# Hybrid layer projects residual times norm weights, rstd applied behind PSUM; small projections in column tiles; key sums in four units; turns later

## The chip, the cores and the metric

The kernel runs on one core of a Trainium2 chip. The metric is device time in microseconds (us) of one execution, inputs in HBM, outputs in HBM; lower is better. Engines in the text: PE is TensorE, DVE is VectorE, ACT is ScalarE, POOL is GpSimd, SP is SyncE, which issues the DMAs.

## The reference

Two networks run one after the other on 256 tokens of width 1024 in fp32. The first has two layers (attention, a gating unit, a dilated attention) and isn't touched. The second puts 16 meta tokens ahead (272 tokens) and has two layers, each: half a SwiGLU FFN, a mixer, half a SwiGLU FFN. Layer 0's mixer is the hybrid one:

```python
h = h + 0.5 * swiglu_ffn(rms_norm(h, ffn_norm[0, 0]), ...)
hn = rms_norm(h, mix_norm[0])          # x * rsqrt(mean(x*x) + 1e-6) * gain
# in the mixer:
fq, fk, fv, ff, gqkv, ga, gb, gz = split_cols_2(hn @ w_in, HYB_SIZES)
o_fox = forgetting_attention(...)       # 8 heads of 64, decay from ff
gqkv = silu(causal_depthwise_conv(gqkv, conv_w)); k, q l2-normalised
o_gdn = gated_delta_rule(...)           # 4 heads of 128, decay from ga, beta from gb
o = concat([o_fox, rms_norm(o_gdn, o_gain) * silu(gz)]);  h = h + o @ w_out
```

The columns `ff`, `ga`, `gb` (8 + 4 + 4) are the small projections. Layer 1's mixer is a recurrence (rwkv) and keeps its form. Since rms_norm multiplies each token by one number (rstd), `hn @ w` is also `(x * gain) @ w` times rstd of the token.

## The kernel before, in words

Everything is held transposed: channels on the 128 partitions in KC = 8 chunks, tokens (272 or 256) in the free dimension. Weights come as blocks of 128x1024 (512 KB) through a ring of RING = 4 slots. Each block is split into a high and a low part (`act_split`: a copy on ACT in two halves of 128x512; `dve_split`: the subtraction on DVE), two blocks (SPLIT = 2) ahead of PE: the half for block n waits until PE has finished the same half of block n - 2. Activations are split in the same way (`act_parts`, `dve_parts`). `pe_tile` (L424) then does one 128x128 tile as three matmuls, L426 to L428; a block is 8 tiles, 24 matmuls.

Each engine runs its own hand-written order, and semaphores join them. Around the change:

- The FFN's last two blocks finish their 8 output banks one by one; `dve_ffn_add` adds each to the residual X.
- `act_norm`, `pe_norm`, `dve_mean`, `act_rstd`, `dve_norm` (L529 to L592): squares on ACT, their sum by fp32 matmuls with ones, mean, Ln, Exp, then the normed chunks H. Then the parts MIX_H, MIX_L, and then PE's first block of the hybrid layer.
- FFN stages don't wait for that: their opening (`pe_open` L599, `act_open`, `dve_open`, L598 to L674) multiplies the residual times gain, takes the first two blocks in halves (PAIR: first half of both, then second half of both), and each product is multiplied by rstd when it leaves PSUM. `OPEN` lists the norms that do this (numbers 3, 5, 6, 8: the four FFNs). The first FFN has no adds or splits to weave in and takes another path in the two helpers.
- The hybrid layer: `pe_hybrid_in`, `act_hybrid_in`, `dve_hybrid_in` (L1826, L1943, L2157) are loops over HYB_CH = 28 blocks i, and after `if i == ...` stands the other work of that turn: small projections (i = 2), their rows through log, scan and spread (3 to 7), convolutions (`dve_convolve`, on DVE), key and query sums (10, 11), grams, an inverse by levels (`ax`, `xax`, 14 to 19), the delta rule by chunks (20 to 26), the forgetting attention (`fox_*`, 18 to 26). ACT copies each block's result from one of two PSUM banks to HP (L1948).
- `pe_mix_out` then projects OUT_H, OUT_L, and an FFN follows.

Of the kernel before, what the change touches and what calls it, by code (L numbers as in the profile page):

```python
# [22 lines left out]
ALU = mybir.AluOpType  # L23
# [3 lines left out]
P = 128  # L27
D = 1024
KC = D // P
# [54 lines left out]
def _columns(table):  # L84
# [11 lines left out]
    ("delta_rows", 8 * P), ("delta_cols", 8), ("chunk_mask", 2 * len(R_WIDTHS)), ("restart", S2), ("row_scan", S2),  # L96
# [12 lines left out]
    ("ffn_g", DEPTH * 2 * KC), ("mix_g", DEPTH * KC), ("final2_g", KC), ("hyb_small", KC * T2),  # L109
# [6 lines left out]
def host_constants():  # L116
# [58 lines left out]
    put("delta_rows", sel)  # L175
    put("delta_cols", cut)
# [11 lines left out]
def host_vectors(i, first):  # L188
# [26 lines left out]
    small = np.zeros((D, T2), np.float32)  # L215
    small[:, 0:8], small[:, 32:36], small[:, 64:68] = w[:, 1536:1544], w[:, 3080:3084], w[:, 3084:3088]
    put("hyb_small", small.reshape(KC, P, T2).transpose(1, 0, 2).reshape(P, -1))
# [52 lines left out]
def build(nc, x_in, pos_in, const_in, first_in, vec_in, weights_in, out):  # L270

    ctx = ExitStack()
    with ctx:
# [245 lines left out]
        NORMED = {use: j for j, use in enumerate((0, 1, 2, 4, 7, NORMS))}  # L519
        OPEN = (3, 5, 6, 8)  # L520
# [97 lines left out]
        def act_open(act, job, use, x, n, gain, high, first):  # L618
# [192 lines left out]
        def pe_fox_weigh(pe, j):  # L811
            pe.wait_ge(fox["turned_taken"], max(FOX_AT["pair", j], FOX_AT["tail", j // 2]) + 1)
            if j:
                pe.wait_ge(act_low, KC * JOBS["hybrid", 1] + j)
            for o in range(2):
                h, out_ = 2 * j + o, PS[64 * o:64 * o + 64, 4, 0:S2]
                v, last = FVN[:, :, 64 * h:64 * h + 64], FOX_TAIL * (h % 4) + FOX_TAIL - META
                tail = FOX_TAIL_T[:, j // 2]
                nc.tensor.matmul(out_[:, 0:256], v[:, 0], FOX_T[:, j % 2, o, 0:256], start=True, stop=False)
                nc.tensor.matmul(out_[:, 128:256], v[:, 1], FOX_T[:, j % 2, o, 256:384], start=False, stop=True)  # L820
                nc.tensor.matmul(out_[:, 256:S2], v[:, 0], tail[:, last:last + META], start=True, stop=False)
                nc.tensor.matmul(out_[:, 256:S2], v[:, 1], tail[:, P + last:P + last + META], start=False, stop=False)
                mm = nc.tensor.matmul(out_[:, 256:S2], v[0:META, 2], tail[0:META, 2 * P + last:2 * P + last + META],
                                      start=False, stop=True)
# [170 lines left out]
        def dve_setup(dve):  # L995
            ang, turns, ang2 = arena(SCR, S1), arena(SCR + 256, S1), arena(SCR + 512, S1)
# [633 lines left out]
        HYB_BANKS, GRAM_BANK = 2, 5  # L1630

        def pe_hybrid_block(pe, i):
            block, _ = BLOCKS["mix_in", 0]
            pe_arrived(pe, block + max(i, 1))
            if i >= HYB_BANKS:
                pe.wait_ge(hs["in_taken"], i - HYB_BANKS + 1)
            for k in range(KC):
                if i == 0:
                    pe.wait_ge(act_low, KC * JOBS["hybrid", 0] + k + 1)
# [1443 lines left out]
```

## Time and profile before

| | |
|---|---|
| median of 3 runs | 2021.8 us (2021.31 to 2022.74) |
| the profiled execution | 2023.71 us, span 2021.9 us |
| PE busy | 1894.4 us, 94% |
| DVE busy | 1279.0 us, 63% |
| ACT busy | 1033.5 us, 51% |
| granted TensorE clock, mean | 0.973 of full |
| DMA | 278.13 MB, 138 GB/s |

PE's matmuls overlap, so its rows last longer (0.29 us) than they stand apart (0.126 us at the full clock, 0.227 at half). One row of a fp32 matmul by ones or by a constant is one of two passes. The hybrid layer lies from 854 to about 1050 us of the span; the FFN openings are at 654, 1079, 1282 and 1818 us.

### The profile page before, as it was taken

The numbers are of one execution on the slowest core, as the hardware profiler recorded it, in microseconds if no ns is written. First come the engines' busy times: TensorE is split into PE (matmuls) and PEld (weight loads), VectorE is DVE, ScalarE is ACT, GpSimd is POOL, SyncE is SP. The second block draws the span as 40 slices with busy tenths as digits, with TensorE's granted clock in tenths as the row PEclk, the third lists the DMA queues.
The fourth block names the chain that finished last, engine by engine and source line by source line (L and its number), as shares of the span: only waits on it lengthen the run. The fifth ranks groups of instructions, "written<-read, shape, count | busy, mean of one in ns | idle before, by whom it ended". The sixth has DMA issues, their size and how long they took to land.

```text
span 2021.9 us, 46291 instructions
## 1 busy us (share of the span) xinstructions
PE 1894.4 (94%) x17922; PEld 1805.1 (89%) x17922; DVE 1279.0 (63%) x2593; ACT 1033.5 (51%) x2037; POOL 25.4 (1%) x20
## 2 busy tenths in 40 slices
PE   5999998999997999989999999999989978979998
PEld 5989988989997999988889999899976978869998
DVE  4667675667666666476456664566566755467764
ACT  4555654555654555447355554555445723155553
POOL 0110000110000000000000000000000000000000
PEclk8999998999998999989999999999989989989999
DMA  5544554544553555532225555455542400025664
GB/s 224 154 137 146 156 177 126 157 141 142 159 174 117 168 174 176 164 90 93 64 64 162 170 176 177 144 170 176 177 161 82 127 31 4 4 73 168 186 187 125
DMA packets 75531, 278.13 MB, mean 138 GB/s; under 512 B 8320, under 2 KB 9600, under 8 KB 74752
## 3 DMA queue, kind: packets, MB, share of 16 engines
q1 hardware_dynamic: 75392, 276.12, 44.4%
q8 instruction: 106, 1.74, 0.3%
q14 instruction: 33, 0.27, 0.0%
HBM read 275.04 MB, written 1.05 MB: 137 GB/s over the span
## 4 chain that ended last, share of the span: by engine, by line
PE 81%; DVE 11%; ACT 5%; issue 2%; DMA 0%; DVEq 0%; SPq 0%; ACTq 0%
PE psum L426 22%; PE psum L427 21%; PE psum L428 21%; DVE weights_low L391 3%; ACT weights_high L383 2%; PE psum L2669 1%; PE psum L2652 1%; PE psum L720 1%; PE psum L1750 1%; PE psum L2666 1%; PE psum L564 1%; PE psum L740 1%; PE psum L2610 1%; DVE normed L589 1%; PE psum L2357 1%
## 5 line engine op out<-in xcount | busy, mean ns | idle before, releaser
L391 DVE TENSOR_TENSOR weights_low<-weight_ring,weights_high 128x512 fp32r<-128x512 f32 x996 | 673.9, 692 | 536.0 <-ACT weights_high L383 526.8
L383 ACT ACTIVATE weights_high<-weight_ring 128x512 fp32r<-128x512 f32 x996 | 615.2, 628 | 603.7 <-PE psum L428 601.6
L426 PE MATMUL psum<-ffn_normed_high,weights_high 128*128 128x272 f32 (+1 forms) x1408 | 407.8, 290 | 13.3 <-DVE ffn_normed_low L652 10.0
L428 PE MATMUL psum<-ffn_normed_high,weights_low 128*128 128x272 f32 (+1 forms) x1408 | 405.4, 288 | 0.0
L427 PE MATMUL psum<-ffn_normed_low,weights_high 128*128 128x272 f32 (+1 forms) x1408 | 405.3, 288 | 0.0
L426 PE MATMUL psum<-first_normed_high,weights_high 128*128 128x256 f32 x1216 | 355.6, 292 | 29.8 <-DVE first_normed_low L445 17.7
L427 PE MATMUL psum<-first_normed_low,weights_high 128*128 128x256 f32 x1216 | 342.7, 282 | 0.0
L428 PE MATMUL psum<-first_normed_high,weights_low 128*128 128x256 f32 x1216 | 342.4, 282 | 0.0
L426 PEld LDWEIGHTS psum<-ffn_normed_high,weights_high 128*128 128x128 f32 x1408 | 266.8, 189 | 17.7 <-issue 11.7
L426 PEld LDWEIGHTS psum<-first_normed_high,weights_high 128*128 128x128 f32 x1216 | 233.6, 192 | 44.7 <-issue 26.6
L428 PEld LDWEIGHTS psum<-ffn_normed_high,weights_low 128*128 128x128 f32 x1408 | 266.7, 189 | 0.0
L427 PEld LDWEIGHTS psum<-ffn_normed_low,weights_high 128*128 128x128 f32 x1408 | 266.3, 189 | 0.1
L427 PEld LDWEIGHTS psum<-first_normed_low,weights_high 128*128 128x128 f32 x1216 | 233.4, 192 | 2.1 <-issue 1.9
L428 PEld LDWEIGHTS psum<-first_normed_high,weights_low 128*128 128x128 f32 x1216 | 233.3, 192 | 0.0
L426 PE MATMUL psum<-ffn_inner_high,weights_high 128*128 (+2 forms) x704 | 201.9, 287 | 1.0 <-DVE weights_low L391 0.5
L428 PE MATMUL psum<-ffn_inner_high,weights_low 128*128 (+2 forms) x704 | 201.3, 286 | 0.0
L427 PE MATMUL psum<-ffn_inner_low,weights_high 128*128 (+2 forms) x704 | 201.1, 286 | 0.0
L426 PEld LDWEIGHTS psum<-ffn_inner_high,weights_high 128*128 128x128 f32 x704 | 132.5, 188 | 2.6 <-DVE weights_low L391 1.6
L428 PEld LDWEIGHTS psum<-ffn_inner_high,weights_low 128*128 128x128 f32 x704 | 132.4, 188 | 0.0
L427 PEld LDWEIGHTS psum<-ffn_inner_low,weights_high 128*128 128x128 f32 x704 | 132.4, 188 | 0.0
L1482 ACT ACTIVATE arena<-arena 128x272 f32<-128x272 f32 (+1 forms) x88 | 37.7, 429 | 96.7 <-DVE arena L1518 96.7
L426 PE MATMUL psum<-mixer_high,weights_high 128*128 128x272 f32 x224 | 69.8, 312 | 5.4 <-DVE mixer_low L445 5.4
(423 smaller groups left out, 2891.4 us busy)
## 6 DMA issues: line engine op xcount, KB each, us to landing
weight_ring<-weights_in SPq DMA_DIRECT2D x508, 512.0 KB, 3.7
arena<-first_in SPq DMA_DIRECT2D x1, 2176.0 KB, 13.8
consts<-const_in SPq DMA_DIRECT2D x1, 1828.5 KB, 17.7
arena<-vec_in SPq DMA_DIRECT2D x1, 1536.0 KB, 9.3
arena<-vec_in SPq DMA_DIRECT2D x1, 1152.0 KB, 5.9
residual<-x_in SPq DMA_DIRECT2D x1, 1088.0 KB, 5.2
out<-normed SPq DMA_DIRECT2D x4, 256.0 KB, 2.5
vectors<-vec_in SPq DMA_DIRECT2D x1, 399.0 KB, 6.6
```

What stands on the lines that cost most here:

```text
L383: nc.scalar.activation(WH[:, n % SPLIT, half], W[:, n % RING, half], ACT.Copy).then_inc(weights_high, 1)
L391: nc.vector.tensor_tensor(WL[:, n % SPLIT, half], W[:, n % RING, half], WH[:, n % SPLIT, half].bitcast(F32), ALU.subtract).then_inc(weight ...
L426: nc.tensor.matmul(psum, WH[:, s, cols], high, start=start, stop=False)
L427: nc.tensor.matmul(psum, WH[:, s, cols], low, start=False, stop=False)
L428: return nc.tensor.matmul(psum, WL[:, s, cols], high, start=False, stop=stop)
L564: mm = nc.tensor.matmul(PS[:, bank, 0:n], ONES, SQ[:, k, 0:n], start=(k == 0), stop=(k == KC - 1))
L589: nc.vector.scalar_tensor_tensor(out=dest[:, k, 0:n], in0=x[:, k], scalar=gain[:, k:k + 1], in1=RS[:, 2, 0:n], op0=ALU.mult, op1=ALU.mult)\
L720: mm = nc.tensor.matmul(A.score(h, m, qi), q[r, c, qi * A.t:(qi + 1) * A.t], k[r, c, 0:w], start=True, stop=True)
L740: mm = nc.tensor.matmul(PS[o:o + A.e, A.out_bank(h), kj * A.t:A.n], v[0:A.t, kj, h * A.e:(h + 1) * A.e], A.probs_t(h, kj), start=(kj == 0) ...
L1482: nc.scalar.activation(FFN_GATE[:, u, 0:n], FFN_GATE[:, u, 0:n], ACT.Silu).then_inc(gates_silu, 1)
L1750: mm = nc.tensor.matmul(inv_psum(g, part)[half(o), m - m0], left[half(o), m], right[half(o), m], start=True, stop=True)
L2357: mm = nc.tensor.matmul(PS[row:row + width, bank, 0:S2], LI[:, k, at:at + width], x[:, k], start=(k == 0), stop=(k == KC - 1))
```

## The change

- The hybrid layer's norm joins `OPEN` (number 4). PE projects X times gain without waiting for the norm: `pe_open` for blocks 0 and 1, then the small projections from X, then the sum. rstd is multiplied in by DVE as it takes each block out of PSUM (`dve_hybrid_take`); ACT's copies are gone. The first four blocks use banks 0, 1, 5, 6, later ones 0 and 1.
- The small projections' weights are 32 columns wide (they were 68), multiplied by the gain once in `dve_setup`, and go to four column tiles; a constant matrix `small_rows` adds the four and puts them on their rows.
- The order in `act_open` and `dve_open` is another, for the FFNs too: adds ahead of parts, two squares earlier, splits paired.
- Key and query sums go in four units of two chunks.
- `pe_fox_turn` comes after `pe_delta_xax` (i = 19) and after `pe_delta_u` (i = 20); DVE normalises the tail first. `pe_fox_weigh` alternates the two column halves. Convolutions 0 and 1, the memset of UN and the gates stand at other turns.

```diff
-    ("ffn_g", DEPTH * 2 * KC), ("mix_g", DEPTH * KC), ("final2_g", KC), ("hyb_small", KC * T2),
+    ("ffn_g", DEPTH * 2 * KC), ("mix_g", DEPTH * KC), ("final2_g", KC), ("hyb_small", KC * 32),
...
-        NORMED = {use: j for j, use in enumerate((0, 1, 2, 4, 7, NORMS))}
-        OPEN = (3, 5, 6, 8)
+        NORMED = {use: j for j, use in enumerate((0, 1, 2, 7, NORMS))}
+        OPEN = (3, 4, 5, 6, 8)
...
-            for k in range(3):
-                part(k)
-                square(k)
+            part(0)
+            square(0)
+            part(1)
             act_split_half(act, first, 0, 0)
+            part(2)
+            act_split_half(act, first, 1, 0)
+            square(1)
             part(3)
-            act_split_half(act, first, 1, 0)
-            square(3)
-            for k in range(4, 7):
-                part(k)
+            square(2)
+            part(4)
+            part(5)
             act_split_half(act, first, 0, 1)
+            act_split_half(act, first, 1, 1)
+            part(6)
             part(7)
-            act_split_half(act, first, 1, 1)
-            for k in range(4, KC):
+            for k in range(3, KC):
                 square(k)
...
-            for k in range(3):
-                add(k)
+            add(0)
+            for k in range(2):
+                add(k + 1)
                 part(k)
             add(3)
             dve_split_half(dve, first, 0, 0)
             add(4)
+            add(5)
+            part(2)
             dve_split_half(dve, first, 1, 0)
             part(3)
-            add(5)
             add(6)
+            part(4)
+            add(7)
             dve_split_half(dve, first, 0, 1)
-            add(7)
-            part(4)
-            dve_split_half(dve, first, 1, 1)
             for k in range(5, KC):
                 part(k)
+            dve_split_half(dve, first, 1, 1)
...
         def dve_setup(dve):
+            small = vec("hyb_small").rearrange("p (k c) -> p k c", k=KC)
+            dve_chain.later(nc.vector.tensor_tensor(small, small, vec("mix_g", 0, KC).unsqueeze(2).broadcast_to([P, KC, 32]), ALU.mult))
...
+        def hybrid_bank(i):
+            return (0, 1, 5, 6)[i] if i < 4 else i % 2
...
-            if i >= HYB_BANKS:
-                pe.wait_ge(hs["in_taken"], i - HYB_BANKS + 1)
+            if i >= 4:
+                pe.wait_ge(hs["in_taken"], i - 3 if i < 6 else i - 1)
...
             for k in range(KC):
-                mm = nc.tensor.matmul(PS[0:T2, 7, 0:S2], small[:, k], H[:, k], start=(k == 0), stop=(k == KC - 1))
+                rows = slice(32 * (k % 4), 32 * (k % 4) + 32)
+                mm = nc.tensor.matmul(PS[rows, 7, 0:S2], small[:, k], X[:, k], start=(k < 4), stop=(k >= 4))
             mm.then_inc(hs["small_ready"], 1)
+
+        def pe_small_rows(pe):
+            pe.wait_ge(hs["z_ready"], 1)
+            nc.tensor.matmul(PS[0:T2, 7, 0:S2], const("small_rows"), ROWS[:, 2], start=True, stop=True).then_inc(hs["small_ready"], 1)
...
+        def pe_sums(pe, m):
+            pe.wait_ge(hs["squares"], 2 * m + 2)
...
+            if m == 3:
                 pe.wait_ge(hs["sums_taken"], 1)
...
+            for j in range(2):
+                mm = nc.tensor.matmul(PS[:, 2 + 2 * (m % 3) + j, 0:S2], ONES, SQ[:, 2 * m + j], start=True, stop=True)
...
-        def pe_hybrid_in(pe, normed):
-            for i in range(HYB_CH):
+        def pe_hybrid_in(pe, norm):
+            block, _ = BLOCKS["mix_in", 0]
+            pe_open(pe, block, ("hybrid", 0), norm, S2, MIX_H, MIX_L, (0, 1), HYB_SUMS)
+            pe_small(pe)
+            pe_open_sum(pe, norm, S2, HYB_SUMS)
+            for i in range(2, HYB_CH):
                 pe_hybrid_block(pe, i)
                 if i == 2:
-                    pe_small(pe, normed)
+                    pe_small_rows(pe)
...
+                    pe_delta_xax(pe, 4)
                     pe_fox_turn(pe, "pair", 0)
-                    pe_delta_xax(pe, 4)
                 if i == 20:
                     pe_delta_w(pe)
                     pe_fox_scores(pe, "pair", 1)
+                    pe_delta_u(pe, 0)
                     pe_fox_turn(pe, "tail", 0)
-                    pe_delta_u(pe, 0)
...
             for i in range(HYB_CH):
                 act_split(act, block + i + SPLIT)
-                act.wait_ge(blocks_done, block + i + 1)
-                nc.scalar.activation(HP[:, HYB_STREAM[i]], PS[:, i % HYB_BANKS, 0:S2], ACT.Copy).then_inc(hs["in_taken"], 1)
+                if i == 1:
+                    act_rstd(act, norm, S2)
...
+        def dve_hybrid_take(dve, i):
+            block, _ = BLOCKS["mix_in", 0]
+            dve.wait_ge(blocks_done, block + i + 1)
+            nc.vector.tensor_tensor(HP[:, HYB_STREAM[i]], PS[:, hybrid_bank(i), 0:S2], RS[:, 2], ALU.mult).then_inc(hs["in_taken"], 1)
...
+                if i == 0:
+                    dve_partial_sums(dve, norm, S2, HYB_SUMS)
                 if i == 1:
-                    dve_convolve(dve, 0)
+                    dve_mean(dve, norm, S2, HYB_SUMS, 32 * D)
+                    dve.wait_ge(rstd_ready, norm + 1)
+                    dve.wait_ge(hs["small_ready"], 1)
+                    nc.vector.tensor_tensor(ROWS[:, 2], PS[:, 7, 0:S2], RS[:, 2], ALU.mult).then_inc(hs["z_ready"], 1)
+                    dve_hybrid_take(dve, 0)
+                if i and not 15 <= i <= 19 and not 21 <= i <= 24:
+                    dve_hybrid_take(dve, i)
...
                     nc.vector.tensor_scalar(t, t, 1.0, None, ALU.add).then_inc(hs["z_ready"], 1)
-                    dve_convolve(dve, 1)
+                    dve_convolve(dve, 0)
...
                     nc.vector.tensor_tensor_scan(ROWS[0:T2, 3], const("row_scan", T2), sp, 0.0, ALU.mult, ALU.add).then_inc(hs["rows_ready"], 1)
+                    dve_convolve(dve, 1)
```

## Rows read from the trace of the kernel before

**Rows 1.** The page, engines; PE's waits from 640 us on (us in total, times, longest)

```profile
PE 1894.4 (94%) x17922; PEld 1805.1 (89%) x17922; DVE 1279.0 (63%) x2593; ACT 1033.5 (51%) x2037; POOL 25.4 (1%) x20
...
PE psum L426 <- DVE ffn_normed_low L652: 10.0, 5, 6.1
```

**Rows 2.** PE in order of time, 854 to 879 us: start, us, what, [idle <-releaser]

```profile
853.99 3.37 PE L564 MATMUL psum<-squares,consts 128*128 128x272 f32 x14
...
863.72 0.57 PE L426 MATMUL psum<-mixer_high,weights_high 128*128 128x272 f32 x1 [5.45 <-DVE mixer_low L445]
...
872.01 0.29 PE L428 MATMUL psum<-mixer_high,weights_low 128*128 128x272 f32 x1
...
875.17 3.83 PE L1649 MATMUL psum<-normed,vectors 128*68 128x272 f32 x16
...
878.63 0.49 PE L426 MATMUL psum<-mixer_high,weights_high 128*128 128x272 f32 x1
```

**Rows 3.** PE in order of time, opening of the third FFN

```profile
1281.79 0.29 PE L428 MATMUL psum<-ffn_inner_high,weights_low 128*128 128x272 f32 x1
...
1289.27 0.60 PE L426 MATMUL psum<-ffn_normed_high,weights_high 128*128 128x272 f32 x1 [1.10 <-DVE ffn_normed_low L652]
...
1293.36 1.12 PE L611 MATMUL psum<-squares,consts 128*32 128x272 f32 x16
```

**Rows 4.** DVE in order of time: adds, half splits, parts, product with rstd

```profile
849.14 0.96 DVE L1559 SCALAR_TENSOR_TENSOR residual<-psum,residual 128x272 f32<-128x272 f32 x2
...
852.63 1.29 DVE L407 TENSOR_TENSOR weights_low<-weight_ring,weights_high 128x512 fp32r<-128x512 f32 x2 [1.02 <-ACT weights_high L402]
...
853.85 1.13 DVE L1559 SCALAR_TENSOR_TENSOR residual<-psum,residual 128x272 f32<-128x272 f32 x3
...
1288.72 1.32 DVE L652 SCALAR_TENSOR_TENSOR ffn_normed_low<-residual,vectors,ffn_normed_high 128x272 fp32r<-128x272 f32 x3
...
662.47 0.44 DVE L1518 TENSOR_TENSOR arena<-psum,rstd 128x272 f32<-128x272 f32 x1 [0.96 <-ACT rstd L559]
```

**Rows 5.** PE in order of time, opening of the second FFN, first row and end

```profile
1078.58 0.29 PE L426 MATMUL psum<-ffn_normed_high,weights_high 128*128 128x272 f32 x1
...
1085.65 1.12 PE L611 MATMUL psum<-squares,consts 128*32 128x272 f32 x16
```

**Rows 6.** PE in order of time, the hybrid layer's waits at turns 5, 10, 11

```profile
889.82 0.50 PE L1654 MATMUL psum<-arena,consts 68*128 68x272 f32 x1 [1.75 <-DVE arena L2180]
...
914.79 2.10 PE L1690 MATMUL psum<-squares,consts 128*128 128x272 f32 x8 [0.83 <-ACT squares L1941]
...
921.82 2.07 PE L1690 MATMUL psum<-squares,consts 128*128 128x272 f32 x8 [1.90 <-ACT normed L1930]
```

**Rows 7.** Stretches: length, each engine's busy time (x), PEclk, DMA share, GB/s

```profile
893.00:894.00 1.00, 1.00 (x6) 1.00 (x6) 0.96 (x3) 0.00 (x0) 0.00 (x0) 0.50 0.39 156
...
866.00:929.90 63.90, 59.42 (x408) 54.82 (x407) 45.32 (x102) 37.42 (x71) 0.00 (x0) 0.95 0.35 105
```

**Rows 8.** PE in order of time, the two attention turns that waited, and the work behind one

```profile
980.40 0.33 PE L806 MATMUL psum<-consts,arena 128*128 128x128 f32 x1 [1.74 <-DVE arena L867]
...
981.21 2.20 PE L1750 MATMUL psum<-arena 64*64 64x64 f32 x40
...
992.49 0.55 PE L803 MATMUL psum<-consts,arena 128*128 128x128 f32 x3 [1.76 <-DVE arena L867]
```

**Rows 9.** PE in order of time, column halves: alternating, one after the other, next work

```profile
932.11 1.04 PE L1726 MATMUL psum<-consts,arena 128*64 128x128 f32 x16
...
998.56 0.65 PE L819 MATMUL psum<-arena 128*64 128x256 f32 x2
...
1000.95 0.65 PE L1786 MATMUL psum<-arena 64*64 64x128 f32 x8
```

**Rows 10.** PE in order of time, the first output projection's wait

```profile
1054.72 0.39 PE L426 MATMUL psum<-mixed_high,weights_high 128*128 128x272 f32 x1 [1.25 <-DVE mixed_low L2291]
```

**Rows 11.** PE in order of time, start of the kernel

```profile
8.32 5.57 PE L564 MATMUL psum<-squares,consts 128*128 128x256 f32 x16 [8.32 <-DMA vectors<-vec_in]
```

More of the change, by code:

```diff
@@ L175, in host_constants @@
     put("delta_rows", sel)
+    rows = np.zeros((P, T2), np.float32)
+    for j in range(4):
+        for r in range(16):
+            rows[32 * j + r, r if r < 8 else r + 24 if r < 12 else r + 52] = 1.0
+    put("small_rows", rows)
     put("delta_cols", cut)
@@ L814, in pe_fox_weigh @@
                 pe.wait_ge(act_low, KC * JOBS["hybrid", 1] + j)
+            out_ = [PS[64 * o:64 * o + 64, 4, 0:S2] for o in range(2)]
+            v = [FVN[:, :, 64 * h:64 * h + 64] for h in (2 * j, 2 * j + 1)]
+            last, tail = [FOX_TAIL * (h % 4) + FOX_TAIL - META for h in (2 * j, 2 * j + 1)], FOX_TAIL_T[:, j // 2]
             for o in range(2):
[L816 to L823, printed above, removed]
+                nc.tensor.matmul(out_[o][:, 0:256], v[o][:, 0], FOX_T[:, j % 2, o, 0:256], start=True, stop=False)
+            for o in range(2):
+                nc.tensor.matmul(out_[o][:, 128:256], v[o][:, 1], FOX_T[:, j % 2, o, 256:384], start=False, stop=True)
+            for o in range(2):
+                nc.tensor.matmul(out_[o][:, 256:S2], v[o][:, 0], tail[:, last[o]:last[o] + META], start=True, stop=False)
+            for o in range(2):
+                nc.tensor.matmul(out_[o][:, 256:S2], v[o][:, 1], tail[:, P + last[o]:P + last[o] + META], start=False, stop=False)
+            for o in range(2):
+                mm = nc.tensor.matmul(out_[o][:, 256:S2], v[o][0:META, 2], tail[0:META, 2 * P + last[o]:2 * P + last[o] + META],
                                       start=False, stop=True)
@@ L1681, in pe_fox_rows @@
                                  start=True, stop=True).then_inc(hs["spread"], 1)
-        def pe_sums(pe, g):
-            pe.wait_ge(hs["squares"], 4 * g + 4)
-            if g:
+        def pe_sums(pe, m):
+            pe.wait_ge(hs["squares"], 2 * m + 2)
+            if m == 0:
+                pe.wait_ge(hs["fox_rows"], 5)
+            if m == 3:
                 pe.wait_ge(hs["sums_taken"], 1)
-            else:
-                pe.wait_ge(hs["fox_rows"], 5)
-            for j in range(4):
-                mm = nc.tensor.matmul(PS[:, 2 + j, 0:S2], ONES, SQ[:, 4 * g + j], start=True, stop=True)
+            for j in range(2):
+                mm = nc.tensor.matmul(PS[:, 2 + 2 * (m % 3) + j, 0:S2], ONES, SQ[:, 2 * m + j], start=True, stop=True)
             mm.then_inc(hs["sums"], 1)
@@ L1973, in act_hybrid_in @@
                     load_log_exp(act)
[L1974 to L1976 removed]
+                if i in (10, 11):
+                    act_key_root(act, 2 * i - 20)
+                    act_key_root(act, 2 * i - 19)
                 if i == 13:
@@ L2196, in dve_hybrid_in @@
                     dve_convolve(dve, 4)
+                if i == 10:
+                    dve_chain.later(nc.vector.memset(UN, 0.0))
                 if i == 11:
@@ L2215, in dve_hybrid_in @@
                 if i == 20:
+                    dve_fox_normalise(dve, "tail", 0)
                     dve_fox_lowest(dve, "pair", 1)
-                    dve_fox_normalise(dve, "tail", 0)
                     dve_delta_un(dve, 0)
@@ L3036, in _ @@
                             continue
-                        dve_norm(dve, norm, X, S2, vec("mix_g", KC * l, KC), H, FFN_OUT[2 * l][0], add, BLOCKS["mix_in", l][0])
                         norm += 1
                         if l == 0:
-                            dve_parts(dve, ("hybrid", 0), H, MIX_H, MIX_L)
-                            dve_hybrid_in(dve)
+                            dve_hybrid_in(dve, norm - 1, add)
                             dve_mix_out(dve, 0, X, S2)
@@ L3044, in _ @@
                         else:
+                            dve_norm(dve, norm - 1, X, S2, vec("mix_g", KC, KC), H, FFN_OUT[2][0], add, BLOCKS["mix_in", 1][0])
                             dve_rwkv_in(dve)
```

79 lines of the change are left out of this document (40 added, 39 removed).

## Prediction

> **What bounds the kernel now.** I read the page first: PE is busy 94% of the span, DVE 63%, ACT 51% [rows 1]. So time is won where PE stands still, runs at half clock, or does work that can be dropped. The waits view, cut to PE, says where it stands still; then I read PE in order of time through the hybrid layer and the FFN openings, and DVE beside it wherever PE waited.
>
> Where the hybrid layer begins, the FFN's last matmul gives way at 853.99 to the fp32 sums of the norm; then comes the chain mean, rstd, eight normed chunks, parts, and PE's first projection starts at 863.72 after 5.45 us of idleness [rows 2]. It starts at half clock: 48 matmuls take to 872.01, 47 spacings in 8.29 us, where the 25 spacings behind them take 3.16, 0.126 each [rows 2]. The third FFN, which has an opening already, also begins behind an FFN, and it shows what an opening costs with the old order: among its waits for DVE's parts is one of 1.10 us, and the matmul behind it lasts 0.60, not 0.29 [rows 3]: half clock again. Inside the hybrid layer PE waits 1.75 us for DVE's scan, then 0.83 and 1.90 us for the key sums [rows 6], and 1.74 and 1.76 us at two attention turns [rows 8].
>
> **The change part by part.** Sums are made against the profiled execution (span 2021.9 us, itself 2023.71); the differences are then taken from the median of the three runs, 2021.8, which the span equals within 0.1.
>
> (A) The opening of the hybrid layer. Before, from the end of the FFN to block 2 of the projection: 853.99 to 872.01 plus one spacing of 0.13, 18.15 us [rows 2]. After: 48 matmuls at full clock, 48 x 0.1255 = 6.0. Sums in four column tiles: sixteen passes in 1.12 [rows 3], of which 1.05 before the next matmul can start. The small projections take the same form, 1.05. One more fp32 product, 0.25. In all 8.35, plus changes of form, 0.1, plus waits. For these I count DVE, the slower helper: from its first add at 849.14 it has 8 adds, 8 parts, 4 half splits. Of several in a row, each costs 0.35, 0.41 and 0.61 (an x3 row of 1.13 less the overlap; likewise 1.32 and 1.29) [rows 4]: 2.8 + 3.3 + 2.4 = 8.5, so done at 857.7. Its last instruction is the half split that PE's last quarter needs, at 853.99 + 4.5 = 858.5. The twelfth, part 3, which the first quarter's last tile needs, comes at about 854.7 (5.1 of work plus some 0.5 for adds that wait for PE's banks); PE gets there at 855.1. In the old order each add, ACT's part and DVE's part stand in a row for the first three chunks, which is what makes DVE late. So nearly no wait; I allow 0.5. New: 9.0, gain 9.2. Lower end: the waits of the third FFN, which takes 11.4 from 1281.92 to 1293.36 in place of 6.0 [rows 3]: gain 4.3. Upper end: no wait, 9.7.
>
> (B) Blocks 2 to 13. The small projections leave PE's path here: 875.17 to 878.63, 3.46 us [rows 2], against two passes with a constant, 0.45: gain 3.0. The log, scan and spread behind them: DVE now also takes blocks 3 and 4 between the split and the scan, at 0.44 each, 0.35 in a row [rows 4], and the rows start 0.2 later behind block 2. PE's wait at turn 5 grows from 1.75 to about 2.7: loss 0.9. The convolution stays between split and scan (0 in place of 1), so it gives nothing. Key sums in four units: the first needs two squares, not four, and the Ln and Exp are half as long, but DVE comes later; I sum to 0.7 + 1.65 of waits in place of 0.83 + 1.90 [rows 6]: gain 0.4. Half clock behind the wait of turn 5 stays (0.50 granted from 893 on [rows 7]). Sum: gain 2.5. Ends: DVE was busy 45.3 of these 63.9 us [rows 7], and twelve takes at 0.35 add 4.2; if every take ended on the path, 4.2 is lost less 0.9 counted: -0.8; if waits don't grow at all, 3.8.
>
> (C) The turn of pair 0 behind `xax`, i = 19. PE waited 1.74 for DVE's normalising [rows 8] and ran the next products at half clock: `xax`, forty small passes, took 2.20 us [rows 8]. Now `xax` at full clock, 1.3 us, covers it, less a take of 0.35 that DVE does before: wait 0.8, gain 0.9, and the half clock goes: 0.9 of `xax`, and about as much of block 20 behind it, together 1.8. Gain 2.7, with 0.9 as lower end if the clock still falls.
>
> (D) The turn of the tail behind `delta_u`, and DVE normalises the tail before the next pair: the product was ready to be made a whole block earlier. The wait of 1.76 [rows 8] goes: 1.8. What is late next is pair 1's turn, a turn later and covered by a block.
>
> (E) `fox_weigh`, four times. One half after the other takes 998.56 to 1000.95, 2.39 us. Sixteen passes of 128 columns that alternate the halves take 1.04 in all, 0.06 each [rows 9]; two passes of 256 columns in one half take 0.65 with their tail of about 0.2, so 0.11 for 128 columns. So alternating products run side by side, and 2.39 becomes 1.2: 4 x 1.15 = 4.6. Ends: 0 and 4.8. The next wait in line is that of `delta_u` for the state that DVE copies; the copy is issued ahead of all this and ends, by DVE's rows, before even the shorter `fox_weigh` does.
>
> (F) The end: the last take is on DVE behind a split, not on ACT, but only one gate is left behind it. PE's wait of 1.25 [rows 10] shrinks by 0.5. Ends 0 and 1.5.
>
> (G) The third FFN's opening takes the new order: 11.4 becomes 6.0 + 0.7: 4.7. Ends 1 and 5.3. (H) The second takes 7.07 from 1078.58 to 1085.65 [rows 5], 6.1 without waits: 0.95; the fourth waits alike: together 1.9. Ends 0 and 2.2. The first FFN takes the other path and stays.
>
> (I) The start. PE's first row waits for the vectors until 8.32 [rows 11]; 288 of their columns are gone, 147 KB, 9% of the three transfers that end there (the page's DMA issues: 1088, 192.5 and 399 KB), so up to 0.7 us. `dve_setup` gets one more product of 256 columns, 0.44 or a little less [rows 4], in the chain that the first projections wait for. Sum 0, ends -0.6 and 0.5.
>
> Sum: 9.2 + 2.5 + 2.7 + 1.8 + 4.6 + 0.5 + 4.7 + 1.9 = 27.9. **2021.8 - 27.9 = 1993.9 us.**
>
> At (A) and (B) the first sums in column tiles start 0.1 later than a neighbour would [rows 3]. The Trainium skill (TensorEngine Tiling, Tiling Modes, Key Properties) says that a change of tiling mode drains TensorE; the change adds two such places. By the row that is 0.2 in all, so the rule speaks against the change and is small here.
>
> **The rivals.**
> R1, the opening is no better than the third FFN's was: the order isn't what makes DVE late, the splits on ACT are. For it: in that opening ACT's splits wait for PE's blocks. Against it: DVE's idle times there stand before its parts, not before its splits. Then A 4.3, G and H 0: 4.3 + 2.5 + 2.7 + 1.8 + 4.6 + 0.5 = 16.4, 2005.4 us.
>
> R2, DVE becomes the bound of the hybrid layer. All 28 results pass through it, where ACT took them. For it: 45.3 busy of 63.9 [rows 7], in order, with three waits of PE on its chain. Against: the convolutions, its longest work, end with block 13. 26 takes x 0.35 on the path: 9.1 lost, 2003.0 us. The Trainium skill (TensorEngine Tiling, PSUM Bottleneck) advises using ScalarE and VectorE both to empty PSUM once TensorE gets faster; the change goes the other way. No row before shows a stage with all of it on DVE but the FFN, where PE doesn't wait for it.
>
> R3, column halves don't overlap in this form (the change doesn't do what it says there): no E, and the small projections and sums longer by 2.4: 27.9 - 4.6 - 2.4 = 20.9, 2000.9 us. [rows 3, 9] speak against it.
>
> R4, slower: DVE is late so often that TensorE is granted 1.2 in place of 2.4 GHz through the middle of the layer, as it was behind the wait of turn 5 (0.50 at 893 [rows 7]). Each block at that clock costs 24 x (0.227 - 0.1255) = 2.4 us more. It decides from twelve blocks on, 29 us; with eighteen, 43 - 27.9 = 15 lost, 2037 us. Against it: waits of 0.83 and 1.90 [rows 6] weren't followed by it.
>
> **How the numbers follow.** Forecast 0.66, with its own range 1989 to 2000 from the ends of A, B, E and G (not all at once). R1 0.13, R2 0.12, R3 0.05, R4 0.04. The range goes down to 1988 (upper ends of A, B, C, G and H: 2021.8 - 33) and up to 2006, past R1 and R2. Faster by more than 0.2% (4 us, about what a measurement of this kernel tells from no change): all but R4 and a mix of R1 and R2 that meets half of R4: 0.95; same 0.01; slower 0.04.
>
> **What would show it.** A: on PE, no idle entry over 0.5 us between the FFN's last matmul and the sums in tiles, block 2 about 8.5 to 9 us behind the FFN, and no half clock. B: the wait before the rows of turn 5 at 2.5 to 3 us; waits at turns 10 to 13 within 2.5 together. C: turn of pair 0 with a wait under 1 us. D: none. E: each `fox_weigh` 1.2 us. G: the third FFN's opening 6.5 to 7. R1 would show waits for parts in all three openings; R2 would show PE's waits released by the takes, from block 4 on. The prediction is wrong most easily in B: the order on DVE is long there, and I have laid it out.

## The result

The changed kernel takes 1994.84 us (median; 1992.78 to 1998.16), the kernel before 2021.72 in the same comparison (2021.31 to 2022.74): ratio 0.9868, 95% interval 0.9851 to 0.9885. 26.9 us are gained, where 27.9 were predicted. A second comparison of the same two gave 1995.84 against 2023.97 (0.9865, 0.985 to 0.988).

The profiled execution of after took 1998.16 us, its span 1996.4, so 25.5 less than the span of before; the sums below are made against that. The page of after, its head and one row of costly groups (columns: busy us, mean ns of one | idle us before them, releaser):

```profile
span 1996.4 us, 46298 instructions
...
PE 1882.1 (94%) x17926; PEld 1796.1 (90%) x17926; DVE 1283.9 (64%) x2616; ACT 1024.4 (51%) x2013; POOL 25.2 (1%) x20
...
L431 PE MATMUL psum<-ffn_normed_high,weights_high 128*128 128x272 f32 (+1 forms) x1408 | 406.3, 289 | 8.7 <-DVE ffn_normed_low L660 6.1
```

The shares say nothing: PE was 94% busy and is. 28 results went from ACT to DVE, yet DVE's busy time grew by 4.9 us only, since the eight products for the normed chunks (3.39 us in before's trace) are gone. The waits for the parts of the FFN's normed chunks fell from 10.0 us in five places to 6.1 in one [rows 1]; that one is the first FFN, which the change leaves alone.

PE in order of time, where the hybrid layer begins (start, us, what, [idle <-releaser]; "..." stands for rows left out):

```profile
854.22 0.28 PE L433 MATMUL psum<-ffn_inner_high,weights_low 128*128 128x272 f32 x1
...
860.49 1.12 PE L616 MATMUL psum<-squares,consts 128*32 128x272 f32 x16
861.43 1.10 PE L1669 MATMUL psum<-residual,vectors 128*32 128x272 f32 x16
862.46 0.72 PE L621 MATMUL psum<-rstd,consts 128*128 128x272 f32 x2
862.83 0.49 PE L431 MATMUL psum<-mixer_high,weights_high 128*128 128x272 f32 x1
```

Nothing carries a bracket: the projection's 48 matmuls follow the FFN's last at 0.13, and block 2 starts 8.48 us after the layer's first matmul (854.35), where it took 18.15 [rows 2].

The waits that are left in the layer and its output projection, with the work at the two turns behind them:

```profile
878.40 2.04 PE L1678 MATMUL psum<-arena,consts 68*128 68x272 f32 x5 [2.64 <-DVE arena L2224]
...
912.14 1.16 PE L1715 MATMUL psum<-squares,consts 128*128 128x272 f32 x4 [0.72 <-ACT normed L1959]
...
921.05 2.40 PE L1729 MATMUL psum<-arena 128*64 128x128 f32 x40 [1.47 <-DVE arena L2143]
...
970.12 0.69 PE L793 MATMUL psum<-arena 64*32 64x272 f32 x8 [1.34 <-DVE arena L2191]
...
971.20 1.38 PE L1775 MATMUL psum<-arena 64*64 64x64 f32 x40
...
973.00 0.33 PE L816 MATMUL psum<-consts,arena 128*128 128x128 f32 x1 [0.42 <-DVE arena L881]
...
976.83 2.00 PE L1800 MATMUL psum<-arena 64*128 64x64 f32 x32
...
980.81 0.55 PE L813 MATMUL psum<-consts,arena 128*128 128x128 f32 x3
981.11 0.37 PE L431 MATMUL psum<-mixer_high,weights_high 128*128 128x272 f32 x1
...
986.10 0.65 PE L829 MATMUL psum<-arena 128*64 128x256 f32 x4
...
987.32 0.65 PE L1811 MATMUL psum<-arena 64*64 64x128 f32 x8
...
1037.13 0.39 PE L431 MATMUL psum<-mixed_high,weights_high 128*128 128x272 f32 x1 [0.86 <-DVE mixed_low L2343]
...
1038.66 0.39 PE L431 MATMUL psum<-mixed_high,weights_high 128*128 128x272 f32 x1 [0.51 <-DVE mixed_low L2343]
```

L1678 spreads the rows, L1715 sums the squares, L1729 makes the grams, L793 is the tail's scores, L1775 is `xax`, L816 pair 0's turn, L813 the tail's turn, L829 to L837 one `fox_weigh`. The wait at 970.12 stands nowhere in [rows 6, 8]: it is new, and its releaser L2191 is `dve_hybrid_take`.

Stretches of after (from and to; length; PE, PE's loads, DVE, ACT, POOL busy with their counts; granted clock, DMA share, GB/s):

```profile
854.30:862.80 8.50, 8.50 (x84) 7.27 (x83) 6.65 (x15) 6.18 (x14) 0.00 (x0) 1.00 0.54 176
862.80:921.00 58.20, 53.41 (x354) 49.20 (x352) 47.77 (x112) 33.63 (x62) 0.00 (x0) 0.91 0.33 103
921.00:1033.00 112.00, 110.18 (x1493) 101.23 (x1494) 68.34 (x196) 54.44 (x142) 0.00 (x0) 1.00 0.23 71
...
881.00:884.00 3.00, 3.00 (x27) 2.28 (x27) 2.93 (x8) 0.62 (x1) 0.00 (x0) 0.50 0.08 11
897.00:898.00 1.00, 1.00 (x7) 1.00 (x6) 1.00 (x4) 0.53 (x1) 0.00 (x0) 0.50 0.00 0
886.00:895.00 9.00, 9.00 (x55) 7.82 (x55) 7.21 (x26) 4.35 (x7) 0.00 (x0) 1.00 0.26 77
1040.00:1042.00 2.00, 2.00 (x11) 2.00 (x11) 1.19 (x3) 1.15 (x2) 0.00 (x0) 0.50 0.43 55
```

The same view of before, over half of the opening and over blocks 2 to 13:

```profile
864.00:869.00 5.00, 5.00 (x24) 5.00 (x24) 3.64 (x8) 0.63 (x1) 0.00 (x0) 0.51 0.01 3
...
872.10:929.90 57.80, 53.32 (x370) 48.72 (x368) 42.44 (x98) 35.25 (x67) 0.00 (x0) 0.97 0.36 107
```

Since the clock that these traces record is either whole or half, a stretch's time at half clock is its length x 2 x (1 - clock): 58.2 x 0.18 = 10.5 us in blocks 2 to 13 of after, 57.8 x 0.06 = 3.5 in before. The clock's own records, which aren't rounded, give 10.2 and 3.4; such sums below are theirs. At half clock the matmuls of before stand 0.227 apart (864 to 868.8 us), at the whole clock 0.1255, so 45% of that time is lost.

The openings of the third and the fourth FFN in after, first matmul and sums (PE in order of time):

```profile
1263.46 0.29 PE L431 MATMUL psum<-ffn_normed_high,weights_high 128*128 128x272 f32 x1
...
1269.60 0.67 PE L616 MATMUL psum<-squares,consts 128*32 128x272 f32 x8
...
1794.28 0.29 PE L431 MATMUL psum<-ffn_normed_high,weights_high 128*128 128x256 f32 x1
...
1800.03 1.07 PE L616 MATMUL psum<-squares,consts 128*32 128x256 f32 x16
```

The fourth in before:

```profile
1818.48 0.29 PE L426 MATMUL psum<-ffn_normed_high,weights_high 128*128 128x256 f32 x1
...
1825.49 1.07 PE L611 MATMUL psum<-squares,consts 128*32 128x256 f32 x16
```

The two traces, stretch by stretch, in us, beside the terms of the prediction (`delta_w` is the row L1800 in after):

| stretch on PE | before | after | gain | predicted |
|---|---|---|---|---|
| A: first matmul of the layer to block 2 | 18.15 | 8.48 | 9.7 | 9.2 |
| B: block 2 to the grams | 57.73 | 58.22 | -0.5 | 2.5 |
| C: grams to `delta_w` | 57.38 | 55.78 | 1.6 | 2.7 |
| D: `delta_w` to the next block | 6.30 | 4.28 | 2.0 | 1.8 |
| E: `fox_weigh`, four | 4 x 2.39 | 4 x 1.22 | 4.7 | 4.6 |
| F: output projection | 28.49 | 28.21 | 0.3 | 0.5 |
| G: third FFN's opening | 11.44 | 6.14 | 5.3 | 4.7 |
| H: second and fourth | 7.07 + 7.01 | 6.14 + 5.75 | 2.2 | 1.9 |

These add to 25.3 of the 25.5 us.

### The profile page after: what moved, and what is told of

Its sections match the earlier page's. It is cut to its first block, busy times and chain, and to the rows that moved or that the text cites. A ratio compares the mean times of both kernels' runs of the same rounds, so it can differ in the third digit from the quotient of the medians.

```text
span 1996.4 us, 46298 instructions
## 1 busy us (share of the span) xinstructions
PE 1882.1 (94%) x17926; PEld 1796.1 (90%) x17926; DVE 1283.9 (64%) x2616; ACT 1024.4 (51%) x2013; POOL 25.2 (1%) x20
## 3 DMA queue, kind: packets, MB, share of 16 engines
HBM read 274.93 MB, written 1.05 MB: 138 GB/s over the span
## 4 chain that ended last, share of the span: by engine, by line
PE 81%; DVE 10%; ACT 6%; issue 2%; DMA 0%; DVEq 0%; SPq 0%; ACTq 0%
PE psum L431 22%; PE psum L433 22%; PE psum L432 21%; DVE weights_low L396 3%; ACT weights_high L388 2%; PE psum L2721 1%; PE psum L2704 1%; PE psum L730 1%; PE psum L2718 1%; PE psum L750 1%; PE psum L569 1%; PE psum L1775 1%; PE psum L2662 1%; PE psum L2409 1%; PE psum L1090 1%
## 5 line engine op out<-in xcount | busy, mean ns | idle before, releaser
L431 PEld LDWEIGHTS psum<-ffn_normed_high,weights_high 128*128 128x128 f32 x1408 | 266.1, 189 | 11.8 <-issue 11.7
```

The source lines that it names most:

```text
L431: nc.tensor.matmul(psum, WH[:, s, cols], high, start=start, stop=False)
```

## The experiments

Theory of the prediction: the openings gain by their order, `fox_weigh` by alternating halves, the turns by standing later, and DVE's order sets the waits of the layer's front. Rivals: ACT's splits set the openings (R1), and DVE's takes are what the layer waits for (R2).

The experiments ran in three later comparisons: e1 to e4 with before at 2024.22, e5 to e8 with before at 2024.46, e9 and e10 with before at 2023.97. After's 1994.84 was measured beside 2021.72. So "over after" and "under after" below, which are differences of medians, carry an offset of up to 2.7 us. Taken by the ratios to before, the distances to after are 12.1 (e1), 3.2 (e3) and 5.1 us (e4) slower, and 6.7 (e5) and 4.2 us (e9) faster, each within about 4.6 either way by the intervals. Where the two ways differ, the stretches of the traces decide.

### e1: the old order in the openings

The changed kernel with the bodies of `act_open` and `dve_open` from before.

```diff
-            add(0)
-            for k in range(2):
-                add(k + 1)
+            for k in range(3):
+                add(k)
                 part(k)
...
```

> The changed kernel, with the order of before put back in the openings (act_open, dve_open), the hybrid layer's opening included; everything else as changed. The theory that the new order is what lets DVE keep up: the hybrid and the third FFN's opening wait as the third FFN's did before (11.4 us in place of 6.1, each 5.3 us), the second and fourth lose 0.9 and 1.2, together 12.7 us more than the changed kernel's 1994.8: 2007.5. Rival, that the opening itself (no norm ahead of it) is the gain and the order adds little: under 3 us more, at most 1998. In the trace the first theory expects waits for the mixer's low parts in the hybrid layer's opening, the rival none.

Measured: 2009.74 us (2006.71 to 2011.64), ratio 0.9928 (0.9914 to 0.9942): 14.9 slower than after. PE in its opening of the hybrid layer:

```profile
855.96 0.39 PE L431 MATMUL psum<-mixer_high,weights_high 128*128 128x272 f32 x1 [0.52 <-DVE weights_low L412]
...
860.91 0.36 PE L431 MATMUL psum<-mixer_high,weights_high 128*128 128x272 f32 x1 [1.28 <-DVE mixer_low L657]
862.62 0.39 PE L431 MATMUL psum<-mixer_high,weights_high 128*128 128x272 f32 x1 [1.10 <-DVE mixer_low L657]
...
867.01 1.12 PE L616 MATMUL psum<-squares,consts 128*32 128x272 f32 x16
```

The waits for DVE's parts are back in the layer's own opening, of the size the third FFN's had [rows 3]: from 855.28 to the sums it takes 11.73 us, in place of 6.14. The four openings lose 13.1 us in the trace (5.6, 0.9, 5.4 and 1.2), where 12.7 were expected. The helpers do the same work in another order, so the order is the cause, and R1's forecast has fallen.

But e1 puts back ACT's order and DVE's together, so it doesn't show that DVE alone was late. In the old order the two wait for each other: in before's third opening ACT stands idle before five of its high parts until DVE has added the chunk (0.60 to 1.11 us each). DVE stands idle three times 0.59 us before a low part, for ACT's high one, and then before two half splits, for ACT's, which stand behind ACT's parts:

```profile
1285.96 0.69 DVE L407 TENSOR_TENSOR weights_low<-weight_ring,weights_high 128x512 fp32r<-128x512 f32 x1 [1.18 <-ACT weights_high L402]
...
1288.11 0.69 DVE L407 TENSOR_TENSOR weights_low<-weight_ring,weights_high 128x512 fp32r<-128x512 f32 x1 [0.70 <-ACT weights_high L402]
```

e1 shows the same 1.18 and 0.70 in the hybrid layer's opening. In after DVE works from 850.53 to 858.45 with no such wait. No run puts back one engine's order alone, so what each of the two is worth stays open.

### e2: only the new order

The kernel before with the two bodies of the changed kernel: the diff of e1 the other way round.

> The kernel before, with only the new order in act_open and dve_open (the FFNs' openings 2 to 4; the hybrid layer has none there). If the gains add up, it gives what the trace of the changed kernel shows for these openings, 5.3 + 0.9 + 1.2 = 7.4 us: 2021.7 - 7.4 = 2014.3. Rival, that the third FFN's opening gained because the stage ahead of it was another: the gain is under 3 us, 2019 or more.

Measured: 2015.31 us (2014.37 to 2015.82) against 2024.22 of before, 0.9958 (0.9945 to 0.9972). The openings of the second and third FFN take 6.14 and 6.13 in its trace, the hybrid layer is as it was (75.94 us from the FFN's end to the grams, 75.88 before). G and H are shown by themselves: 8.9 us by the medians, 7.5 by these stretches of the traces, 6.6 predicted. The order alone, without the layer's new norm, gives a third of the gain.

### e3: one column half after the other

```diff
-            for o in range(2):
-                nc.tensor.matmul(out_[o][:, 0:256], v[o][:, 0], FOX_T[:, j % 2, o, 0:256], start=True, stop=False)
-            for o in range(2):
-                nc.tensor.matmul(out_[o][:, 128:256], v[o][:, 1], FOX_T[:, j % 2, o, 256:384], start=False, stop=True)
...
+            for o in range(2):
+                nc.tensor.matmul(out_[:, 0:256], v[:, 0], FOX_T[:, j % 2, o, 0:256], start=True, stop=False)
+                nc.tensor.matmul(out_[:, 128:256], v[:, 1], FOX_T[:, j % 2, o, 256:384], start=False, stop=True)
...
```

> The changed kernel, with fox_weigh as before: one column half after the other. The theory that alternating halves run side by side and nothing else waits there: 4 x 1.17 = 4.7 us more, 1999.5. Rival, that a shorter fox_weigh only moves the wait to the chain of the delta rule: under 1.5 us more, 1996.3 or less.

Measured: 1999.61 us (1998.23 to 2000.99), 4.8 over after (3.2 by the ratios); `delta_w` to the output projection takes 60.82 in the trace, 56.06 in after's, both without any half clock. These 4.76 us decide. Its `fox_weigh`:

```profile
984.21 0.65 PE L829 MATMUL psum<-arena 128*64 128x256 f32 x2
...
985.41 0.65 PE L829 MATMUL psum<-arena 128*64 128x256 f32 x2
...
986.61 0.65 PE L1807 MATMUL psum<-arena 64*64 64x128 f32 x8
```

Each half costs 1.20, and alternated both together 1.22: R3 has fallen.

### e4: the turns where they were

The changed kernel with `pe_fox_turn` ahead of `pe_delta_xax` and of `pe_delta_u` again, and DVE's `fox_lowest` ahead of the tail's `fox_normalise`.

```diff
-                    pe_delta_xax(pe, 4)
                     pe_fox_turn(pe, "pair", 0)
+                    pe_delta_xax(pe, 4)
...
-                    pe_delta_u(pe, 0)
                     pe_fox_turn(pe, "tail", 0)
+                    pe_delta_u(pe, 0)
```

> The changed kernel, with the two attention turns (pair 0 at i = 19, tail 0 at i = 20) and DVE's order at i = 20 as before. By the changed kernel's rows the move brought 1.6 us at i = 19 and 2.0 at i = 20: 3.6 more, 1998.4. The prediction's own figure was 4.5. Rival, that the wait for take 19, which is new, would be there anyway and covers the turn: then only the 2.0 of i = 20, 1996.8.

Measured: 2001.96 us (2000.5 to 2003.48), 7.1 over after and 5.1 by the ratios, more than all three expectations; the latter is too near the 4.5 to be told from it, but the trace has 6.6. Its waits:

```profile
969.05 0.69 PE L793 MATMUL psum<-arena 64*32 64x272 f32 x8 [1.35 <-DVE arena L2191]
...
971.92 0.33 PE L816 MATMUL psum<-consts,arena 128*128 128x128 f32 x1 [1.73 <-DVE arena L881]
...
984.04 0.55 PE L813 MATMUL psum<-consts,arena 128*128 128x128 f32 x3 [1.77 <-DVE arena L881]
```

The turns' waits are those of [rows 8], to 0.01 us. But they now stand behind the new one of 1.35: grams to `delta_w` is 3.05 us longer than after's, `delta_w` to the output projection 3.53. 3.1 of these 6.6 are waits (1.73 - 0.42 and 1.77), and 3.1 are half clock: from the grams to the output projection e4 has 6.8 us of it (its row below; after's is the third of its stretches, at 1.00). The 4.5 were what the turns cost in the kernel before, where half clock followed one of them only. The stretch of e4, columns as above:

```profile
920.00:1042.30 122.30, 116.95 (x1516) 106.97 (x1516) 71.38 (x201) 57.01 (x148) 0.00 (x0) 0.97 0.22 69
```

### e5: the scan ahead of the convolutions

In the changed kernel the convolutions 0, 1 and 2 each go to a later turn on DVE (0 from i = 3 to 4, behind the scan, 1 to 5, 2 to 6).

```diff
-                    dve_convolve(dve, 0)
                 if i == 4:
...
-                    dve_convolve(dve, 1)
+                    dve_convolve(dve, 0)
                 if i == 5:
-                    dve_convolve(dve, 2)
+                    dve_convolve(dve, 1)
...
                     dve_decays(dve)
+                    dve_convolve(dve, 2)
```

> The changed kernel, with convolution 0 behind the scan (i = 4), 1 at i = 5, 2 behind the decays at i = 6. It takes 3.4 us of DVE's work from ahead of the scan. Theory, the wait of 2.64 us before the rows of turn 5 and the half clock behind it (about 2.7 us in the changed kernel's rows) are what ate the gain of blocks 2 to 13: wait under 0.3 us, no half clock at turn 5, 3 to 5 us less than 1994.8: 1990 to 1992. Rival, DVE is the bound of this stretch and its work is only moved: the wait comes back before the fox rows or at the key sums, and the time stays within 1 us of 1994.8.

Measured: 1990.67 us (1990.36 to 1991.46), 0.9835 (0.9822 to 0.9849), 4.2 under after (6.7 by the ratios), where 3 to 5 were expected. Its waits in the front:

```profile
874.27 2.10 PE L1678 MATMUL psum<-arena,consts 68*128 68x272 f32 x8 [0.36 <-DVE arena L2223]
...
896.75 0.36 PE L431 MATMUL psum<-mixer_high,weights_high 128*128 128x272 f32 x1 [1.36 <-DVE arena L2191]
...
913.88 2.40 PE L1729 MATMUL psum<-arena 128*64 128x128 f32 x40 [0.84 <-DVE arena L2143]
```

The rows' wait falls from 2.64 to 0.36, with it 6.8 us of half clock (10.2 in the stretch, 3.4 left), and 1.36 come back as a new wait, for a take that stands on DVE behind five row copies (2.13 us) and two half splits (1.28). From the layer's first matmul to the grams it takes 61.39, not 66.71. So the order on DVE makes B's loss, not the amount of its work: nothing was taken from it. The 3.4 us of half clock that are left (887.9 to 891.3) begin 13.6 us behind PE's last wait. The stretch from block 2 to the grams in e5, DVE's 47.28 us of work beside after's 47.77:

```profile
861.00:913.90 52.90, 50.34 (x356) 46.66 (x354) 47.28 (x112) 33.13 (x62) 0.00 (x0) 0.97 0.37 114
```

### e6: the take ahead of `delta_ax`

In after's DVE rows the take that releases the wait of 970.12 stands last, behind three products that nobody waits for yet:

```profile
968.16 0.69 DVE L396 TENSOR_TENSOR weights_low<-weight_ring,weights_high 128x512 fp32r<-128x512 f32 x1 [0.76 <-ACT weights_high L388]
968.78 0.94 DVE L2175 TENSOR_TENSOR arena<-psum,consts 128x256 f32<-128x256 f32 x3
969.64 0.43 DVE L2191 TENSOR_TENSOR arena<-psum,rstd 128x272 f32<-128x272 f32 x1
```

```diff
+                if i == 19:
+                    dve_hybrid_take(dve, i)
                 if 15 <= i <= 19:
                     dve_delta_ax(dve, i - 15)
+                if 15 <= i <= 18:
                     dve_hybrid_take(dve, i)
```

> The changed kernel, with take 19 ahead of the masking of the last level, since PE's tail scores wait for it (1.34 us). Theory: that wait goes to under 0.3, the levels' products come 0.35 later, which is covered; 1.0 less, 1993.8. Rival: the turn of pair 0 waits longer in its place (its normalising is behind the same work on DVE) and nothing is gained, 1994.8.

Measured: 1995.21 us (1992.91 to 1997.04). In its trace the wait is 0.49, and grams to `delta_w` takes 54.91, 0.87 less: the place of the take on DVE is shown to cause most of the wait. In the time nothing of it can be seen; the medians of the changed kernel in two comparisons, 1994.84 and 1995.84, differ by as much.

### e7: the small projections in one tile

```diff
-                rows = slice(32 * (k % 4), 32 * (k % 4) + 32)
-                mm = nc.tensor.matmul(PS[rows, 7, 0:S2], small[:, k], X[:, k], start=(k < 4), stop=(k >= 4))
+                mm = nc.tensor.matmul(PS[0:32, 7, 0:S2], small[:, k], X[:, k], start=(k == 0), stop=(k == KC - 1))
```

The constant product behind the passes then reads 32 rows and not 128.

> The changed kernel, with the small projections in one tile of 32 columns, eight in a row, in place of four column tiles side by side; the constant product then reads 32 rows. Theory: sixteen passes take 3.6 in place of 1.05 us, all on PE's path: 2.5 more, 1997.3. Rival, DVE bounds this stretch, so that later work on PE waits less: under 1 us more, 1995.8 or less.

Measured: 1995.27 us (1994.71 to 1997.86): no difference that the time can tell. The sixteen passes in its trace:

```profile
859.61 3.83 PE L1668 MATMUL psum<-residual,vectors 128*32 128x272 f32 x16
```

In four tiles they last 1.10. The layer's first matmul to the grams takes 68.09 us with 6.8 of half clock; e3, with the same 6.8, takes 65.21. So the tiles are worth 2.9 on PE's path in the trace. The median shows 0.4 of it, but e7's runs were granted more clock than after's; the estimate under e10 takes that out and finds 2.4 to 3.0.

### e8: the product of the set-up last

The product of weights and gain goes from the head of `dve_setup` to its end.

> The changed kernel, with the product of the small weights and the gain moved from the head of dve_setup to its end. Theory: 0.4 us less on the chain ahead of the first projections (PE's first FFN row came 0.36 later than before): 1994.4. Rival: the delay is another one, no difference.

Measured: 1997.44 us (1994.76 to 2000.27), 0.9864 (0.9848 to 0.988). Its profile reaches the hybrid layer at 855.96, with 41.0 us of half clock before it; after's reaches it at 854.35 with 34.1. Two other traces with the same half clock before the layer, e4's and e10's, reach it at 854.77 and 855.58. Inconclusive: the 0.4 of term I is smaller than what separates executions that it doesn't reach.

### e9: both orders

e5 and e6 together.

> The scan first (as in e5) and the take of block 19 ahead of delta_ax(4) (as in e6), together. The two lie in different stretches of PE's path (before the grams, and behind them), so they should add: e5's 1990.67 less the 0.87 us that e6's trace showed between grams and delta_w: 1989.8 us, and in the trace layer to grams 61.4, grams to delta_w 54.9. Rival: the take isn't what PE waits for once the front is shorter (DVE then stands as far behind), so grams to delta_w stays at 55.8 and the time at 1990.7.

Measured: 1991.04 us (1989.33 to 1993.81), 0.9847 (0.9833 to 0.986). In the trace they add: 61.40 to the grams and 54.92 from there to `delta_w`, with the take's wait at 0.49 as in e6. In the time e9 is e5 again. Both are faster than the changed kernel: none of their ten runs is above 1993.81, and seven of the eight of after and e10 are; beside e10 itself e9 is 4.8 under.

### e10: the changed kernel once more

> The changed kernel itself, unedited, beside e9 on the same chip. Its own profile again: if the half clock from 896 on that no idle time stands ahead of belongs to the code, layer to grams is 66.7 us again, as in the first profile; if it comes and goes between executions of the same code, 65.2 as in e3 and e4, and the half clock in all differs from 102 us by up to 10. Time 1994.8 within 1.5 either way.

Measured: 1995.84 us (1994.36 to 1999.52). Layer to grams 66.68, with 10.2 us of half clock as in the first profile (66.71), where e3 and e4, with the same code up to there, show 65.21 and 6.8. The waits agree to 0.01. The mean granted clock of e10 and of e9:

```profile
core 0: 1997.8 us, clock 0.973
```

```profile
core 0: 1987.6 us, clock 0.979
```

A mean of 0.973 is 2 x 0.027 x 1998 = 108 us at half clock, and 0.979 is 83. Before the hybrid layer, where of these edits only e8's reaches (e2 is the kernel before), the traces have 34, 37.5 or 41 us of it. A difference of 7 us at half clock is 3 us of time, and the ranges above are of that width.

The record has the mean clock of every run, so the half clock can be taken out, as an estimate: from each time, 0.45 x 2 x (1 - clock) x span. The clock is given to 0.001, which is 1.8 us in one run. The means are then 1953.0 for after and 1952.4 for e10; e3 has 1956.5, e4 1955.6, e7 1955.4 and e8 1951.7. So e7 costs 2.4 to 3.0, as its trace says (2.9); e4 costs 2.6 to 3.2, the 3.1 of its waits; and e8's longer time is the clock's, not the edit's.

## Why the prediction was right

The sum was 27.9 and the difference of medians 26.9 (28.1 in the second comparison). Step by step:

- **A was right in size** (9.2 predicted, 9.7) **and in saying that the order decides.** I had allowed 0.5 of waits and there are none. DVE's last half split of the opening ends at 858.45 in after's trace (laid at 857.7), still before PE's last quarter begins (854.35 + 4.5); e1 shows that the order alone stands between this and 11.7 us. The sums in tiles and the small projections took 0.94 and 1.03 up to the next row, 1.05 each predicted. What was read wrong is how the old order makes DVE late. The prediction says that DVE's idle times stand before its parts and not before its splits, and that ACT's splits wait for PE's blocks. In before's rows 1.88 of DVE's 3.65 us of idleness stand before half splits (shown under e1), and ACT's four splits of that opening follow its parts with no wait for PE. The gain came from freeing both engines, not from DVE's list alone.
- **G and H were a little low** (6.6 predicted, 7.5 in the trace), for the same reason: no wait of the allowed 0.7 is left.
- **B is the term that was mis-sized most: 2.5 predicted, -0.5 measured**, which is near its stated lower end of -0.8. Its waits came out as laid out: 2.64 for the rows (2.7 predicted), 0.72 and 1.47 for the key sums and behind them (0.7 and 1.65). The step that failed is "Half clock behind the wait of turn 5 stays". In before, that stretch held 3.4 us at 0.50 [rows 7], and the opening ahead of it 6.8 (864 to 869 at 0.51). In after the opening has none, the wait of turn 5 is followed by 6.8 us at 0.50 (879.1 to 885.9), and from 896.1 on by another 3.4. 10.2 - 3.4 = 6.8 more at 45% is 3.1, and 3.0 - 0.9 + 0.5 - 3.1 = -0.5 is the row of the table. In e3, with 6.8 in all, B gives 1.0. By the sums, what A won from the clock was given back in B. Whether the clean opening brought that about, or the wait that grew from 1.75 to 2.64, isn't settled. In e1, whose opening has 3.4 us of half clock, the same wait (2.63) is followed by 3.4 us and not by 6.8. So the wait's length alone doesn't set it, though e1 is one trace. e5 takes most of the wait away and gets 5.3 us in the trace (3.8 against e3's), 4.2 in time. The stretch from block 2 to the grams in e3, where after's has 0.91:

```profile
862.40:919.10 56.70, 51.83 (x354) 47.77 (x352) 47.76 (x112) 33.63 (x62) 0.00 (x0) 0.94 0.34 106
```

- **C was mis-sized too: 2.7 predicted, 1.6 measured.** The turn's wait fell to 0.42 (0.8 predicted) and `xax` ran at full clock, 1.38 for 2.20 [rows 8]. The missed step is the tail's scores: they wait for block 19's result, which ACT used to copy at once; now DVE takes it behind `delta_ax`, 1.34 us late. The turn's wait gives 1.3, the 3.4 us of half clock that are gone give 1.5, and the new wait takes 1.3: 1.5 of the 1.6 measured. I had counted the take that stands before the turn, not the one before the scores.
- **D, E and F** came as worked out: 2.0, 4.7 and 0.3 for 1.8, 4.6 and 0.5. e3 shows E in the trace, 4.76. e4 says that C and D together are worth 6.6 in the trace and not 4.5 inside the changed kernel: without the move, the new wait and the old ones stand close together, and 6.8 us of half clock come with them.
- **R2 was true in small.** Two waits released by takes were seen, 1.34 in after and 1.36 in e5; R2 had all the takes on the path. DVE's load is not what bounds the layer, but the order in which it takes costs time. The Trainium skill (TensorEngine Tiling, PSUM Bottleneck) would share the emptying of PSUM between ScalarE and VectorE. No run here shares them. The traces give two takes of 28, one in after and one in e5, that stood behind other work while PE waited; for the others DVE alone was enough.
- **R4** did not come: in after, waits of 0.72, 1.47 and 1.34 were not followed by half clock, that of 2.64 was, and so were the two short ones of the output projection, 0.86 and 0.51 (3.4 us from 1039.5). The same two were followed by none in e3 to e7 and e9, so from a wait's length it can't be told.
- **I** stayed open (e8).
- **The ends of the range** don't all follow. B's upper end is 3.4 by its own terms (3.0 + 0.4), not 3.8. C has no upper end that is worked out; even with 3.8 for B, those of A, B, G and H and the rest as forecast add to 30.6, not 33, so the bound would have been 1991, not 1988. The measured time lies inside either way.

The total was close partly by luck, because the misses cancel: B and C gave 4.1 less than predicted, A, D, E, F, G and H together 1.5 more, and the medians lie 1.4 further apart than the two spans.

## What to carry to other kernels

When a norm's scale is moved behind PSUM, the opening gave its full gain here only with both helpers' work in an order in which neither waits for the other and PE's tiles find their parts: lay the rows of both out with their durations, add for add and split for split, before anything is moved. When an evacuation goes to a busier engine, list every reader of each result, not the average load: one of 28 takes stood behind work that nobody waited for yet, and a convolution stood ahead of the scan that PE waited for. Count half clock over the whole stretch and the next one, in both kernels: here the opening lost 6.8 us of it and the blocks behind it got 6.8 more. And compare with a run of the same comparison, or in the traces: medians of one kernel in different comparisons lay up to 2.7 us apart.

## What the runs showed of the hardware

- Half clock without a wait of PE's just ahead of it. In after PE was busy 9.00 us of 9.00 from 886 to 895 at 1.00, and at 897 the granted clock was 0.50 (above), 17.7 us behind PE's last wait; e8 and e10 have it at the same place, while e3 and e4 had the same instructions there and 1.00. What brings it on isn't settled. The PE work of that stretch is partly small fp32 products.
- The changed kernel has 100 us of half clock in one trace and 107 in another, without an edit; with its one-edit variants it is 89 to 109, some 9 us of time at 45%, of which the edits account for a part. Medians moved with it, e8's by 2.6 us. Effects under 3 us could be told here from traces alone, or with the clock taken out.
- Alternating two column halves in fp32 makes both as fast as one: 1.22 (after) against 1.20 for one half (e3). Sixteen passes over four column tiles last 1.10; in one tile, 3.83 (e7).
